# Sample attention over a paged cache: two groups of eight pages in flight on TensorE, VectorE, ScalarE and SyncE in place of one

## What is computed

```python
def fox_sample(k_past, v_past, logf_past, q, k, v, logf):
    ...
    s_past = jnp.einsum('bqhd,bkhd->bhqk', q, k_past).astype(F32) * scale + g[..., :, None] + suffix[..., None, :]
    s_new = jnp.einsum('bqhd,bkhd->bhqk', q, k).astype(F32) * scale + g[..., :, None] - g[..., None, :]
    ...
    p = jax.nn.softmax(jnp.concatenate([s_past, s_new], axis=-1), axis=-1).astype(v.dtype)
    return (jnp.einsum('bhqk,bkhd->bqhd', p[..., :n_past], v_past)
            + jnp.einsum('bhqk,bkhd->bqhd', p[..., n_past:], v))
```

## Time and profile before

| | |
|---|---|
| median of 3 runs | 2553.26 us (2551.98 to 2556.07) |
| the profiled execution's own time | 2555.88 us |
| its span in the trace | 2554.0 us |
| granted TensorE clock, mean | 0.886 of full |
| sample attention in the trace | first score at 374.91 us, last output added from 1196.94 us |

### The profile page before, as it was taken

How to read it: one execution, slowest core, us unless ns; L and a number is a source line. 1 busy time by engine, 2 the same in 40 slices (tenths; PEclk the granted TensorE clock), 3 DMA queues, 4 the chain that set the end, 5 groups by cost and what they waited for, 6 DMA issues and landing times.

```text
span 2554.0 us, 41115 instructions
## 1 busy us (share of the span) xinstructions
PE 2039.9 (80%) x16723; PEld 1529.0 (60%) x16723; DVE 1094.5 (43%) x1979; ACT 321.0 (13%) x785; POOL 197.4 (8%) x266
## 2 busy tenths in 40 slices
PE   6998865455555555555899999999999889999996
PEld 4776643333333333334677777777777667777774
DVE  4323644444444444445443344533234543335443
ACT  2003520000000000000112210011110111220002
POOL 1003100000000000000100012220000110002221
PEclk9998987777667677677999999999999899999998
DMA  4121037677676777764111221231110111212211
GB/s 145 66 95 61 1 127 254 243 241 255 224 257 224 246 246 243 248 237 162 66 66 66 73 93 66 82 114 35 66 68 28 51 66 69 97 66 75 91 66 37
DMA packets 127992, 320.44 MB, mean 125 GB/s; under 512 B 10236, under 2 KB 10514, under 8 KB 127678
## 3 DMA queue, kind: packets, MB, share of 16 engines
q1 hardware_dynamic: 124258, 304.67, 33.8%
q0 software_dynamic: 3296, 12.98, 1.5%
q10 hardware_dynamic: 252, 0.16, 0.0%
HBM read 309.20 MB, written 8.55 MB: 124 GB/s over the span
## 4 chain that ended last, share of the span: by engine, by line
PE 78%; DVE 17%; ACT 2%; issue 2%; DMA 0%; DVEq 0%; ACTq 0%; SPq 0%
PE ps L852 44%; DVE work L1879 9%; PE ps L1052 8%; PE ps L1074 5%; PE ps L1149 2%; PE ps L1150 2%; PE ps L1062 2%; DVE stats L1894 2%; ACT work L1450 2%; PE ps L774 1%; PE ps L775 1%; PE ps L1001 1%; PE ps L803 1%; PE ps L804 1%; DVE work L1904 1%
## 5 line engine op out<-in xcount | busy, mean ns | idle before, releaser
L1052 PE MATMUL ps<-work,big 32*32 32x256 f32 x6144 | 191.7, 556 | 256.5 <-DVE work L1879 252.7
L1052 PEld LDWEIGHTS ps<-work,big 32*32 32x32 f32 x6144 | 133.8, 129 | 312.8 <-DVE work L1879 266.5
L852 PE MATMUL ps<-xn,wring 128*128 128x288 f32 x1104 | 295.8, 412 | 20.0 <-DVE xn L1598 15.7
L852 PE MATMUL ps<-work 128*128 128x288 f32 x1152 | 296.4, 411 | 11.9 <-DVE work L1645 7.8
L852 PEld LDWEIGHTS ps<-work 128*128 128x128 f32 x1152 | 222.0, 193 | 75.0 <-issue 12.8
L852 PEld LDWEIGHTS ps<-xn,wring 128*128 128x128 f32 x1104 | 212.1, 192 | 80.6 <-issue 20.1
L852 PE MATMUL ps<-big,wring 128*128 128x288 f32 x944 | 252.8, 412 | 7.6 <-DVE big L2142 7.6
L1879 DVE STREAM_TRANSPOSE work<-work 128x768 f32<-128x768 f32 x256 | 222.5, 935 | 0.0
L852 PEld LDWEIGHTS ps<-big,wring 128*128 128x128 f32 x944 | 182.2, 193 | 59.4 <-DVE big L2142 8.5
L1672 DVE TENSOR_TENSOR work<-ps,work 128x288 f32<-128x288 f32 x72 | 32.9, 457 | 320.5 <-PE ps L852 320.5
L707 POOL TENSOR_TENSOR h<-h,xn 128x288 f32<-128x288 f32 x96 | 106.0, 1107 | 812.6 <-DVE xn L1679 698.1
(11 more groups left out here) (348 smaller groups left out, 2507.9 us busy)
## 6 DMA issues: line engine op xcount, KB each, us to landing
work<-in_cache_k SPq DMA_DIRECT2D x256, 384.0 KB, 5.6
big<-in_cache_v SPq DMA_DIRECT2D x256, 384.0 KB, 5.4
wring<-in_w_up SPq DMA_DIRECT2D x16, 2048.0 KB, 7.5
wring<-in_w_down SPq DMA_DIRECT2D x16, 2048.0 KB, 7.9
wring<-in_w_in_odd SPq DMA_DIRECT2D x6, 2048.0 KB, 8.0
wring<-in_w_in_even SPq DMA_DIRECT2D x5, 2048.0 KB, 13.8
wring<-in_w_out_even SPq DMA_DIRECT2D x2, 2048.0 KB, 7.9
wring<-in_w_out_odd SPq DMA_DIRECT2D x2, 2048.0 KB, 7.9
```

The costliest lines, as they stand in the source:

```text
L852: last = mm(bank, w[:, k, :], x[:, k, :], start=k == 0 and not onto, stop=k == 3, skip_group_check=onto)
L1052: last = mm(ps[32 * c:32 * c + 32, 4 + q, 0:256], w, x, start=(n == 0), stop=(n == 2 * HC))
```

## The change

The work of a group is kept and put into other places of the lists, so that two groups are in flight.

- VectorE turns the pages of group g+1 in the list of group g: three before `shift_group(g)`, one behind it, four behind the addition of group g-1 and the next bias.
- TensorE weighs pages 0 to 3 of a group before the next group's scores and pages 4 to 7 behind them. All eight turns of the probabilities are made at once, in columns 256 to 511 of banks 4 to 7, and ScalarE, not VectorE, copies them to SBUF with one instruction (`take_probs`).
- SyncE issues K page n and V page n - 8 in turn, one behind the other, where it issued eight K pages and then eight V pages.
- The new tokens have a place of their own in bank 2 (`new_psum`) and the turned outputs another (`out_psum`). Their steps are spread over the third and the fourth group of a sequence, and the counting functions are gone. Denominator and decay of a group have two places, by g % 2.

The core of the diff:

```diff
@@ stats and PSUM places @@
-        den_s, group_den, decay, group_max, rec_s = (lambda b, n=n: stat(b, n) for n in (4, 5, 6, 7, 8))
+        den_s, group_max, rec_s = (lambda b, n=n: stat(b, n) for n in (4, 7, 8))
+        group_den, decay = (lambda g, n=n: stat(g // GS, n + 4 * (g % 2)) for n in (5, 6))
+        new_psum = ps[:, 2, 0:192]
+        out_psum = ps[:, 2, 192:448]
@@ @blk.sync @@
-            for g in range(NG):
-                for n in range(g * GP, (g + 1) * GP):
-                    if n % 4 == 0:
-                        ids = page_ids(n)
-                    if n == 8:
-                        sp.wait_ge(sem("pool_d_ready"), 1)
-                    if n >= KSLOTS:
-                        sp.wait_ge(sem("scored"), (n - KSLOTS) // GP + 1)
-                    sp.dma_start(k_ring[:, k_slot(n), :], rows_of("cache_k", ids[n % 4])).then_inc(k_in[k_slot(n)], 16)
-                for n in range(g * GP, (g + 1) * GP):
-                    if n % 4 == 0:
-                        ids = page_ids(n)
-                    if n >= VSLOTS:
-                        sp.wait_ge(sem("v_page_used"), n - VSLOTS + 1)
-                    sp.dma_start(v_ring[:, n % VSLOTS, :], rows_of("cache_v", ids[n % 4]))\
-                        .then_inc(v_in[n % VSLOTS], 16)
+            def k_page(n, page):
+                if n == 8:
+                    sp.wait_ge(sem("pool_d_ready"), 1)
+                if n >= KSLOTS:
+                    sp.wait_ge(sem("scored"), (n - KSLOTS) // GP + 1)
+                sp.dma_start(k_ring[:, k_slot(n), :], rows_of("cache_k", page)).then_inc(k_in[k_slot(n)], 16)
+            def v_page(n, page):
+                if n >= VSLOTS:
+                    sp.wait_ge(sem("v_page_used"), n - VSLOTS + 1)
+                sp.dma_start(v_ring[:, n % VSLOTS, :], rows_of("cache_v", page)).then_inc(v_in[n % VSLOTS], 16)
+            for n in range(0, GP, 4):
+                ids = page_ids(n)
+                for m in range(4):
+                    k_page(n + m, ids[m])
+            for n in range(GP, NB * PAGES, 4):
+                k_ids, v_ids = page_ids(n), page_ids(n - GP)
+                for m in range(4):
+                    k_page(n + m, k_ids[m])
+                    v_page(n - GP + m, v_ids[m])
+            for n in range(NB * PAGES - GP, NB * PAGES, 4):
+                ids = page_ids(n)
+                for m in range(4):
+                    v_page(n + m, ids[m])
@@ @blk.tensor @@
-            def turn_half(g, u):
-                if u == 0:
-                    pe.wait_ge(sem("exp_done"), g + 1)
-                pe.wait_ge(sem("turn_taken"), turns_before_group(g) + u)
-                for m in range(4):
-                    at = place(g, 4 * u + m) * P
-                    last = tr(ps[:, 2, m * P:(m + 1) * P], probs[:, at:at + P], ident)
+            def turn_probs(g):
+                pe.wait_ge(sem("exp_done"), g + 1)
+                if g:
+                    pe.wait_ge(sem("probs_in"), g)
+                for at in range(GP):
+                    last = tr(ps[:, 4 + at // 2, 256 + at % 2 * P:256 + at % 2 * P + P], probs[:, at * P:at * P + P],
+                              ident)
                 last.then_inc(sem("probs_turned_s"), 1)
 
             def weigh_page(g, p):
 
                 n = g * GP + p
-                if p % 4 == 0:
-                    pe.wait_ge(sem("probs_in"), 2 * g + p // 4 + 1)
                 if p == 0:
-                    pe.wait_ge(sem("out_added"), outs_before_group(g))
+                    pe.wait_ge(sem("probs_in"), g + 1)
+                    if g:
+                        pe.wait_ge(sem("out_added"), g)
                 pe.wait_ge(v_in[n % VSLOTS], 16 * (n // VSLOTS + 1))
                 for c in range(CG):
                     last = mm(ps[32 * c:32 * c + 32, 3, 0:HC * D], pTs[:, place(g, p), 32 * c:32 * c + 32],
                               v_ring[:, n % VSLOTS, HC * D * c:HC * D * (c + 1)], start=(p == 0), stop=(p == GP - 1))
                 last.then_inc(sem("v_page_used"), 1)
...
+            score_new(0)
+            turn_new(0)
+            weigh_new(0)
             for g in range(NG):
+                b, new = g // GS, g // GS + 1
                 score_group(g)
-                if g % GS == 0 and g:
-                    turn_out(g // GS - 1)
-                for u in range(2):
-                    turn_half(g, u)
-                for p in range(GP):
+                if g:
+                    for p in range(GP // 2, GP):
+                        weigh_page(g - 1, p)
+                if g % GS == GS - 1 and new < NB:
+                    weigh_new(new)
+                turn_probs(g)
+                if g % GS == GS - 2 and new < NB:
+                    score_new(new)
+                for p in range(GP // 2):
                     weigh_page(g, p)
-                if g % GS == GS - 2 and g // GS + 1 < NB:
-                    new_tokens(g // GS + 1)
+                if g % GS == GS - 2 and new < NB:
+                    turn_new(new)
+                if g % GS == 0 and b:
+                    turn_out(b - 1)
+            for p in range(GP // 2, GP):
+                weigh_page(NG - 1, p)
             turn_out(NB - 1)
@@ @blk.scalar @@
                 act.wait_ge(sem("shift_made"), g + 1)
                 if g:
-                    act.wait_ge(sem("probs_turned_s"), 2 * g)
+                    act.wait_ge(sem("probs_turned_s"), g)
                 act_f(probs.rearrange("p (g q k) -> p q g k", g=GP, q=4),
                       ps[:, 4:8, 0:256].rearrange("p q (g k) -> p q g k", g=GP), ACT.Exp,
-                      bias=shift_s(b, n), accum_out=group_den(b)).then_inc(sem("exp_done"), 1)
-                act_f(decay(b), shift_s(b, n - 1), ACT.Exp, bias=shift_s(b, n), scale=-1.0)\
+                      bias=shift_s(b, n), accum_out=group_den(g)).then_inc(sem("exp_done"), 1)
+                act_f(decay(g), shift_s(b, n - 1), ACT.Exp, bias=shift_s(b, n), scale=-1.0)\
...
+            def take_probs(g):
+                act.wait_ge(sem("probs_turned_s"), g + 1)
+                act_f(pTs.rearrange("p (a g) r -> p a (g r)", g=2), ps[:, 4:8, 256:512], ACT.Copy)\
+                    .then_inc(sem("probs_in"), 1)
             exp_new(0)
             for g in range(NG):
                 exp_group(g)
+                take_probs(g)
@@ @blk.vector @@
-            def take_half(g, u):
-                dve.wait_ge(sem("probs_turned_s"), 2 * g + u + 1)
-                if g:
-                    dve.wait_ge(sem("v_page_used"), GP * g)
-                at = place(g, 4 * u)
-                cp(pTs[:, at:at + 4, :], ps[:, 2, :].rearrange("p (g r) -> p g r", g=4)).then_inc(sem("turn_taken"), 1)
-                dve.wait_ge(sem("turn_taken"), turns_before_group(g) + u + 1)
-                dve.sem_inc(sem("probs_in"), 1)
             def add_out(g):
 
                 b = g // GS
                 dve.wait_ge(sem("decay_made"), g + 1)
-                own(stt(den_s(b), den_s(b), decay(b), group_den(b), ALU.mult, ALU.add))
+                own(stt(den_s(b), den_s(b), decay(g), group_den(g), ALU.mult, ALU.add))
                 dve.wait_ge(sem("v_page_used"), GP * (g + 1))
-                dve.wait_ge(sem("out_added"), outs_before_group(g))
+                dve.wait_ge(sem("out_added"), g)
                 o = out_acc[:, b % 2, :]
-                stt(o, o, decay(b), ps[:, 3, 0:HC * D], ALU.mult, ALU.add).then_inc(sem("out_added"), 1)
-            def new_tokens(b):
-                stage_queries(b)
+                stt(o, o, decay(g), ps[:, 3, 0:HC * D], ALU.mult, ALU.add).then_inc(sem("out_added"), 1)
+            def shift_new(b):
                 dve.wait_ge(sem("new_scored"), b + 1)
                 x = probs_new[:, b, NS * b:NS * b + NS]
-                tt(x, ps[:, 2, 0:NS], key_bias[:, NS * b:NS * b + NS], ALU.add).then_inc(sem("turn_taken"), 1)
-                dve.wait_ge(sem("turn_taken"), turns_before_new(b) + 1)
+                own(tt(x, new_psum[:, 0:NS], key_bias[:, NS * b:NS * b + NS], ALU.add))
                 own(nc.vector.reduce_max(neg_max(b, 0), x, AX.X, negate=True))
                 gate = qgate[:, b:b + 1]
                 stt(shift_s(b, 0), neg_max(b, 0), gate, gate, ALU.subtract, ALU.add).then_inc(sem("new_shift_made"), 1)
+            def take_new(b):
                 dve.wait_ge(sem("new_turned"), b + 1)
-                cp(pTn, ps[0:TS, 2, 0:P]).then_inc(sem("turn_taken"), 1)
-                dve.wait_ge(sem("turn_taken"), turns_before_new(b) + 2)
-                dve.sem_inc(sem("new_probs_in"), 1)
+                cp(pTn, new_psum[0:TS, 0:P]).then_inc(sem("new_probs_in"), 1)
+            def start_out(b):
                 dve.wait_ge(sem("new_weighed"), b + 1)
-                cp(out_acc[:, b % 2, :], ps[:, 3, 0:HC * D]).then_inc(sem("out_added"), 1)
+                cp(out_acc[:, b % 2, :], new_psum[:, 0:HC * D]).then_inc(sem("new_added"), 1)
 
...
+            def turn_pages(g, pages):
+                if g < NG:
```

(70 more changed lines are left out.)

28 lines of the change are left out of this document (5 added, 23 removed).

## The result

The changed kernel takes 2378.53 us (median of 4 runs, 2377.24 to 2378.99); the kernel before took 2554.0 us beside it (4 runs, 2551.98 to 2556.07). The ratio is 0.9312, with a 95% interval of 0.9296 to 0.9328: 175 us, or 6.9%, faster. I had forecast 2312, with a range that ended at 2378. The direction was right, and over a quarter of the gain that I had worked out did not come.

What follows compares the result with a forecast made beforehand. Sample attention was bound by an end-to-end chain per group, page turns the largest wait; 31 periods falling from 26.00 to 18.2 us save 241.8, net 241.3, giving 2312 us, range 2264 to 2378.

Steps and rivals of the forecast that it cites:

- Keys, the loop that decides: From a score's end through the last K page's load and turn to the next score's end: 17.9 us, 18.2 with pauses.
- The seventh landing, "10.1": Last K page, seventh of eight loads behind a score, lands 10.1 us after first issue: 7.2 plus three at 0.97.
- The pauses, "0.3": Added to the keys' loop for pauses in scores, which also put the earlier mean period above 24.0 us: 0.3 us.
- The turn and handover, "0.97": VectorE's turn of the last K page before the next score: 6.95/8 = 0.87 us, with 0.1 of handover.
- TensorE's loop, 14.6 to 15.5: TensorE's round of exponentials, probability turns, copy, half the weighing and score: 14.6 us, 15.5 with turns at half clock.
- VectorE under 10: VectorE's page turns, maximum, shift, addition and bias per group: under 10 us of a period of 18.
- SyncE 14.7, transfers 15.5 to 17.2: Per group, SyncE's issues and page-table readings take 14.7 us; sixteen pages take 15.5 at 405 GB/s, 17.2 at 366.
- Transfers become the bound: Rival: page loads at 336 GB/s decide, periods of 18.9 to 20.3 us, 2355 us, DMA share over 0.9; chance 22%.
- Warm queue: Rival: DMA engines already moving, seventh page at 9.0 us, scores 6.0 us; periods 16.1 to 17.3, 2268 us; chance 17%.
- The lists lock into one another: Rival: SyncE's K pages wait behind V slots, VectorE's maximum behind K pages; periods of 21 to 24, 2429 us; chance 9%.
- Slower by alternating: Rival: reading two caches alternately lowers the rate, below 242 GB/s decides; at 230, 27.3 us periods, 2594 us; chance 2%.
- The signs of being wrong: Prediction fails if rate is well under 345 GB/s, seventh page takes over 11 us, or an unlisted wait appears.

Runs made afterwards that it cites:

- Run 8: Against the changed kernel, SyncE's old order of issue restored, eight K pages and then eight V pages: 2411.38 us, ratio 0.944.
- Run 4: Against the changed kernel, only the first half of each V page's columns loaded (heads 6 to 11 not the reference's): 2318.0 us, ratio 0.9088.
- run 1: Against the changed kernel, SyncE issues four K pages and then four V pages instead of alternating them: 2288.01 us, ratio 0.8969.
- Run 10: Against the changed kernel, sixteen K slots, four K pages ahead of four V, only 32 of 768 V columns loaded from page 16 on: 2230.08 us, ratio 0.8726.
- Run 5: Against the changed kernel, sixteen K slots in place of twelve and four K pages issued ahead of four V pages: 2266.61 us, ratio 0.8867.
- run 2: Against the changed kernel, sixteen K slots in place of twelve, with K and V pages still alternating: 2357.19 us, ratio 0.9241.

## Why the prediction was right in direction and too fast

**The bound before** held. The page turns and the exponentials were what TensorE waited for, and 152 us of these two waits went.

**Keys, the loop that decides: right mechanism, mis-sized term.** I had 0.14 + 10.1 + 0.97 + 6.72 + 0.3 = 18.2. Measured: 11.48 + 1.06 + 7.80 = 20.34. The 2.1 us that are missing are these:

- *The seventh landing, "10.1": +1.24 with the 0.14 in front.* This is the step that failed first. I took four landings of one group before (7.2) and added three pages at the rate of the fullest stretch. Behind the scores of after the loads land at 3.4, 5.1, 7.0, 8.1, 9.2, 10.4 and 11.5 us on the mean. The fourth is 0.7 later than my 0.14 + 7.2: 0.1 because the group that I had read was a quick one (the mean before was 7.44), the rest because of something in the new order. Run 8, with four K pages in that place, has 7.63; why two V pages of the same size among the four cost 0.4 more, and where the last 0.2 comes from, is open. The three others took 1.14 us each and not 0.97. SyncE had issued the seventh by 3.8 us, so its issues were not what was late. Run 4 prices the V pages ahead, run 1 takes them away: 2.8 us earlier, 90 us.
- *The pauses, "0.3": +0.8.* I took pauses over from before as they were. They came to 28.8/31 = 0.93 us a period inside scores, which I read as instructions being used faster when TensorE's waits go (the part on the pauses above; not shown by an edit). Without its pauses a score takes 7.80 - 0.93 = 6.87, near my 6.72. TensorE stayed at half clock through most of it (granted 0.50 from 514 to 518 us), as I had kept.
- *The turn and handover, "0.97": +0.09.* A page turned alone takes 0.98 us, not 6.95/8 = 0.87 as in a run of eight.

**TensorE's loop, 14.6 to 15.5:** right. Run 10, where little else decides, has 15.48, with 1.3 of pauses in it and about 1 of waiting for turned pages. ScalarE's copy, for which I took 1.1, took 1.02; the wait for it is 1.0 us in each group. The wait for the exponentials is 1.2 us a group, not under 1.

**VectorE under 10:** it is busy for 330.8/31 = 10.7 us a period (turns at 0.98), still far from deciding. Its maximum starts 0.03 us behind the score in the group shown; the strict list did no harm.

**SyncE 14.7, transfers 15.5 to 17.2:** neither decided in after. Run 5 ran at 374 GB/s over 500 us with a share of 1.00, which makes 6.29 MB in 16.8 us: between my two rows, and a full stage does not keep the 405 of a stretch of 8 us. The Trainium skill (SBUF — State Buffer, Summary: rules for kernel authors) reckons with about 358 GB/s, which makes an estimate of 17.6 us a group; run 5 moved 4% more than that, so the trace does not agree.

**The rivals.** *Transfers become the bound* forecast 2355, the nearest number, by another mechanism: the share was 0.85, not over 0.9, and run 1 took 90 us off with every byte still moved. What was slow was the order and the restart. Two of this rival's reasons were right all the same, and my own loop should have had them: pages behind a score do not land 0.97 us apart (the seven of after 1.35 on the mean), and the wait for the score does open a hole. Its periods, 18.9 to 20.3, ended at the one measured. *Warm queue* did not come: the DMA engines had almost run dry when a score ended (in the group shown nothing was issued from 512.91 to 521.27 us; over 31 groups their mean share is 0.15 in the last 0.5 us of a score and 0.02 from 0.5 to 1.0 us behind it). *The lists lock into one another* had a chance of 9%. The time of after does not need it, since the K slots close at the same point, but it is real: run 2 shows it with 152.9 us of waits for V slots, and came 80 to 125 us short of what I had expected there. In run 5, where these waits are 55.7 us, 91 us of it came. *Slower by alternating* did not come: after moved 310 GB/s with both caches in turn, far above the 242 that it needed, and run 8, with eight and eight, is 33 us slower, though through weighing's wait and not through the rate.

**The signs of being wrong** that I had put down did show. The seventh page landed 11.3 us after the first issue, over my 11, which is the sign that names the cause. The rate was 310 GB/s and not 345, but that says little by itself: 6.29 MB in 20.34 us are 309. TensorE waited 5.4 us a period for turned pages and not 3.

**The end:** the last score starts at 1005.1 and what follows took its time as forecast; all of the result lies in the periods.

## What to carry to other kernels

When a load moves onto the deciding loop, count the bytes that stand ahead of it in the issue list, not only its own latency, and put what the loop waits for first: putting four K pages ahead of four V pages gave 90 us more here, over half of what the whole pipeline had given. A queue issued in order by one engine joins all its waits: more slots for one stream (21 us) or the other (none) give little until the list's order and both sets of slots fit. Landings behind a restart should be read as a mean over many groups; one group and the rate of one full stretch were together 1.2 us too kind, which times 31 is 38 us.

## What the runs showed of the hardware that I had not expected

- TensorE seems to run short of instructions. At 224 small matmuls (32x32 by 32x256) with as many weight loads in some 7 us, pauses of up to 4.6 us appear inside a run of matmuls, 200 of the 209 of 0.8 us or more with a read of 16,384 bytes on queue q8, kind "instruction", that ends 1.2 to 1.6 us before work goes on. With those in weighing they rose from 6 us before to 35 in after and 74 in run 5, where they are the largest wait of TensorE.
- After a pause of the queue the first page lands 3.4 us after the score's end, and the next two come 1.7 and 1.9 us apart before the steps fall to 1.1. Why is open. In run 5, whose queue stays full, the step between landings has a median of 0.97 us and a mean of 1.06.
- A full queue held 374 GB/s for 500 us on one core, and 405 for 8 us.
